# The recurrence's output turned over GpSimd's queue; gate bias and causal mask prepared by GpSimd and added by VectorE in the maximum's instruction

## The chip, the cores and the metric

The kernel runs on one core of one Trainium2 chip. The metric is the device time of one execution in microseconds (us). The engines are TensorE (PE in the rows), VectorE (DVE), ScalarE (ACT), GpSimd (POOL) and SyncE (SP), whose queue issues most DMAs.

## The reference, cut to what matters

One sequence of 256 tokens, 1024 features, float32, goes through two blocks. The second holds two token mixers side by side. The recurrence's output `o_a` is normed, multiplied with a gate and multiplied by `w_branch_a`. The other mixer is causal attention of 8 heads of width 128 with a forget gate, and the change is mostly there:

```python
c = cumsum(log_sigmoid(f_logit))            # per token and head
s = (q @ k.T) / sqrt(128) + c[query] - c[key]
s = where(key <= query, s, -inf)
p = softmax(s)                              # c[query] falls out: it is the same for a whole row
o_b = p @ v
```

So the scores of head h need one value per key, -c[key], the same for every query, and the mask.

## The kernel before, in words

Tokens lie in two tiles of 128 (`TT`); within the first tile they are in reverse order. Every weight matrix is cut into units of 128 x 2048 values, 6 slots deep. For each unit SyncE loads `raw` in two DMAs (L603), ScalarE rounds it to `high` (L1365), VectorE takes `rest` = raw - high (L1961), and TensorE does 24 products of 512 columns from them (L817 to L819 or L854 to L856), three per pair of operands. TensorE works units in a fixed order, and the other engines run programs written out by hand that name, for each unit u of the block `win2` (36 units, j = u // 2 names the product), what is done there besides. `load(u)` on SyncE first waits until unit u - 6 is used (L598); after the weights it does the small transfers listed for that unit (L604 to L608), in order, each with its wait.

A tensor is "turned" in two steps: VectorE transposes it in blocks of 32 x 32, one DMA stores it in DRAM, four DMAs read it back with the blocks exchanged (`turn`, L643).

**The attention.** At u = 7 VectorE scans the gate logits to `fcum` (40 rows; rows 0 to 7 and 32 to 39 both hold the 8 heads), clears `fbias` (L2531) and signals `fcum_ready`. At u = 8 ScalarE copies `fcum` to `fbias` in a rounded form (L1739) and VectorE puts the remainder into rows 32 to 39 (L2607). Head n is in unit u = 26 + n (`FOX_SLOT`). In `fox(n)` TensorE spreads row n and its remainder over all partitions by a product of the two-hot matrix `identr` with `fbias` (L1173, 384 columns), adds the mask by a product of the identity `identb` with `causal` (L1175, 256 columns in bf16), and adds the scores in L1178. Both are accumulated in one bank of PSUM. VectorE reduces each tile to its negated maximum (L2553, 128 and 256 columns), ScalarE exponentiates with it as bias and sums (L1811), VectorE divides at the start of the next unit (`fox_scale`, L2083 to L2089) and blocks `fpT`, which SyncE turns (L663, L667), and in `fox(n + 3)` TensorE multiplies with the values (L1186, L1187); VectorE takes the result to `fo` (L2635).

In each unit u of this stretch VectorE's order is: `fox_scale` of the head before, `rest` of unit u + 4, the maximum, the gate (L2597, odd units from 29), the second half of the output's turn (L2632, units 32 and 34), `fo`. ScalarE's is: `high` of unit u + 4, the tanh of the gate (L1770), the rounding of the turned output (L1803, units 32 and 34), the exponentials.

**The recurrence's output.** At u = 28 and 30 VectorE transposes token tile 0 and 1 from `hg` to `oa_squares` (L2640). SyncE stores each (L648) and reads it back into `hg` (L654), at `load(34)`, `load(35)` and `load(36)`, `load(37)` of the block. ScalarE makes `at_high`, VectorE `at_rest` (L2632), and TensorE waits for both tiles of `at_rest` (`oa_rest`, L1224) before the first unit of `brA`. The gate of the second branch takes the place of `oa_squares`, so VectorE waits until it is stored (L2594).

**GpSimd** issues the small loads on a queue of its own, and takes differences for the recurrence (L742 to L763), the last at some 605 us. Then it waits until the last head's product is done (L797), loads `mem` (L798) and the gains.

Of the kernel before, what the change touches and what calls it, by code (L numbers as in the profile page):

```python
# [222 lines left out]
def build(nc, dram, out_dram):  # L223
    ctx = ExitStack()
    with ctx:
# [29 lines left out]
        for name, shape, dt in (  # L255
            ("ident", [P, P], F32), ("identb", [P, P], BF16), ("causal", [P, TT, P], BF16),
# [3 lines left out]
            ("meanvar", [P, TT, 2], F32), ("identr", [P, HH], F32R), ("eps", [P, 2 + 2 * TT], F32), ("negmax", [P, HH, 2], F32),  # L260
# [3 lines left out]
        identr = small["identr"]  # L264
        partsum = small["eps"][:, 2:2 + 2 * TT].rearrange("p (a t) -> p a t", a=2)
        ident, identb, causal = small["ident"], small["identb"], small["causal"]
# [100 lines left out]
        fbias = place("fbias", [P, P + S], F32R, area + 62 * KB)  # L367
# [35 lines left out]
        mem_turn = (sem("mem_blocked"), [sem(f"mem_stored{n}") for n in range(2)], [sem(f"mem_landed{n}") for n in range(2)],  # L403
# [70 lines left out]
        eps_ready = sem("eps_ready")  # L474
        fox_blocked, fox_stored = sem("fox_blocked"), sem("fox_stored")
# [12 lines left out]
        CONSTS1, CONSTS2 = 8, 4  # L488
# [85 lines left out]
        def _(sync):  # L574
# [16 lines left out]
            def load(u):  # L591
# [16 lines left out]
                turn_probabilities(u)  # L608

# [33 lines left out]
            def turn(u, at, sems, n, home, landing=None, turns=1, ready=None, stored_at=None):  # L643
# [5 lines left out]
                if u == at + 1:  # L649
                    sync.wait_ge(stored[n], stored_at or 16 * turns)  # L650
# [23 lines left out]
            def turn_tokens(u):  # L674

                for tt in range(TT):
                    turn(u, UNIT["win2"] + 34 + 2 * tt, oa_turn, tt, oa_squares[:, tt, :], hg[:, tt, :],
                         stored_at=16 * (tt + 1))
                for tt in range(TT):
                    turn(u, UNIT["brA"] + 9, mem_turn, tt, mem_blocked[:, tt, :])  # L680
                for j in range(2):
                    turn(u, UNIT["brB"] + 7 + 2 * j, y2_turn, j, y2_blocked[j][:, :], stored_at=16 * (j + 1))
                for j in range(2):
                    turn(u, UNIT["mk"] + 7 + 2 * j, mem_turn, j, mk_blocked[:, j, :], turns=2, ready=keys_blocked(j))
# [35 lines left out]
        def _(pool):  # L720
# [15 lines left out]
            pool.dma_start(identb[:, :], dram["c_identb"]).then_inc(consts2_landed, 16)  # L736
# [68 lines left out]
        def _(pe):  # L805
# [364 lines left out]
            def fox(n):  # L1170
                if n < HH:
                    out = aux(("fs", n))
                    pe.matmul(out[:, 0:P + S], identr[:, n:n + 1].to_broadcast([P, P]), fbias[:, :], start=True, stop=False)  # L1173
                    diagonal = out[:, 0:P + S].rearrange("p (n c) -> p n c", n=3)[:, 0:3:2, :]
                    pe.matmul(diagonal, identb[:, :], causal[:, :, :], start=False, stop=False)  # L1175
                    for tt in range(TT):
                        o = out[:, 0:P] if tt == 0 else out[:, P:P + S]
                        mm = pe.matmul(o, fqT[:, n, tt * P:(tt + 1) * P], fox_tokens(fkT, n, *range(tt + 1)), start=False, stop=(tt == TT - 1))  # L1178
# [10 lines left out]
            for u in range(36):  # L1189
# [23 lines left out]
                for n in FOX_SLOT[u]:  # L1213
                    if n == 0:
# [3 lines left out]
                        pe.wait_ge(sem("fcum_rest"), 2)  # L1218
                        pe.wait_ge(consts1_landed, 16 * CONSTS1)
                        pe.wait_ge(consts2_landed, 16 * CONSTS2)  # L1220
# [122 lines left out]
        def _(act):  # L1343
# [379 lines left out]
            for u in range(36):  # L1723
# [12 lines left out]
                if u == 8:  # L1736
                    act.wait_ge(sem("fcum_ready"), 1)
                    for c0, w in ((0, P), (P, S)):
                        act.activation(fbias[0:FROWS, c0:c0 + w], fcum[:, 0:w], ACT.Copy).then_inc(sem("fcum_high"), 1)  # L1739
# [1198 lines left out]
```

## Time and profile before

| | us |
|---|---|
| median of 3 runs | 1052.24 (1051.68 to 1054.19) |
| the profiled execution | 1051.98 |
| its span, first to last instruction | 1050.2 |
| TensorE busy | 1043.2 (99%) |
| VectorE busy | 753.7 (72%) |
| ScalarE busy | 598.4 (57%) |
| GpSimd busy | 68.9 (7%) |
| mean granted TensorE clock | 0.999 of full speed |

Busy time counts an engine's instructions, not its waits. TensorE's products are pipelined: each row lasts longer than its distance to the next, and that distance is what it costs. In rows with a count (x2) the duration is that of all together. "[a <-b]" at the end of a row says that the engine stood idle a us before it, until b was done. The attention's eight heads lie between 631 and 700 us.

### The profile page before, as it was taken

What the parts mean: (1) busy time and instruction counts of PE and PEld (TensorE: products, weight loads), DVE (VectorE), ACT (ScalarE), POOL (GpSimd) and SP (SyncE); (2) the same over time, 40 slices, a digit from 0 to 9 for tenths busy, and PEclk for the clock granted to TensorE, in tenths of its full rate; (3) what the DMA queues carried; (4) which work ended last, traced back from release to release, by engine and by line L of the source; (5) the groups of instructions that cost most, each with busy time, mean ns of one, the idle gap of its engine ahead of it and who ended that gap; (6) DMA issues with size and microseconds to landing.
All of it is one profiled execution on the core that took longest, in us unless ns stands there. A gap on an engine that the chain in (4) does not pass through costs nothing.

```text
span 1050.2 us, 12947 instructions
## 1 busy us (share of the span) xinstructions
PE 1043.2 (99%) x4939; PEld 872.2 (83%) x4939; DVE 753.7 (72%) x901; ACT 598.4 (57%) x800; POOL 68.9 (7%) x59
## 2 busy tenths in 40 slices
PE   9999999999999999999999999999999999999997
PEld 7888888888888888888888888888889988888886
DVE  5768787775787675468888978868778666767642
ACT  6573776765385555448784645555366657565531
POOL 1200000000000000000434500000000000000000
PEclk9999999999999999999999999999999999999999
DMA  9934899985487777648756845979975345878741
GB/s 362 395 131 170 301 303 299 296 264 187 185 280 229 245 239 233 199 177 279 254 179 233 241 161 180 285 247 322 318 250 195 116 171 201 244 239 235 247 158 40
DMA packets 97645, 243.89 MB, mean 232 GB/s; under 512 B 15104, under 2 KB 41904, under 8 KB 97456
## 3 DMA queue, kind: packets, MB, share of 16 engines
q1 hardware_dynamic: 94016, 231.51, 67.4%
q0 software_dynamic: 3136, 11.23, 3.0%
q8 instruction: 39, 0.64, 0.2%
q10 hardware_dynamic: 432, 0.33, 0.1%
q14 instruction: 22, 0.18, 0.0%
HBM read 220.48 MB, written 22.54 MB: 231 GB/s over the span
## 4 chain that ended last, share of the span: by engine, by line
PE 98%; DVE 1%; ACT 0%; issue 0%; DVEq 0%
PE ps L817 24%; PE ps L819 24%; PE ps L818 24%; PE ps L856 5%; PE ps L854 5%; PE ps L855 5%; PE ps L951 1%; PE ps L1141 1%; PE ps L1250 1%; PE ps L1252 1%; PE ps L1251 1%; PE ps L1002 1%; PE ps L1003 1%; PE ps L913 1%; PE ps L914 1%; PE ps L912 1%
## 5 line engine op out<-in xcount | busy, mean ns | idle before, releaser
L1961 DVE TENSOR_TENSOR rest<-raw,high 128x2048 fp32r<-128x2048 f32 x129 | 296.1, 2312 | 75.8 <-ACT high L1365 75.2
L817 PE MATMUL ps<-high,xt_high 128*128 128x512 f32 x824 | 324.4, 394 | 0.2 <-DVE rest L1961 0.2
L818 PE MATMUL ps<-rest,xt_high 128*128 128x512 f32 x824 | 320.8, 389 | 0.0
L819 PE MATMUL ps<-high,xt_rest 128*128 128x512 f32 x824 | 320.8, 389 | 0.0
L1365 ACT ACTIVATE high<-raw 128x2048 fp32r<-128x2048 f32 x129 | 244.4, 1910 | 67.6 <-DMA raw<-in_units_dram 67.5
L817 PEld LDWEIGHTS ps<-high,xt_high 128*128 128x128 f32 x824 | 154.8, 188 | 32.0 <-DVE rest L1961 0.6
L819 PEld LDWEIGHTS ps<-high,xt_rest 128*128 128x128 f32 x824 | 154.7, 188 | 32.1
L818 PEld LDWEIGHTS ps<-rest,xt_high 128*128 128x128 f32 x824 | 154.8, 188 | 31.1
L1966 DVE SCALAR_TENSOR_TENSOR rest<-raw,wgain,high 128x512 fp32r<-128x512 f32 x176 | 119.1, 746 | 35.3 <-ACT high L1369 35.3
L1369 ACT ACTIVATE high<-raw,wgain 128x512 fp32r<-128x512 f32 x176 | 110.9, 716 | 9.1 <-DMA raw<-in_units_dram 9.1
L1625 ACT ACTIVATE act<-ps,recips 128x256 f32<-128x256 f32 x44 | 18.5, 471 | 85.0 <-PE ps L819 85.0
L817 PE MATMUL ps<-high,ht_high 128*128 128x512 f32 x168 | 65.4, 389 | 0.0
L818 PE MATMUL ps<-rest,ht_high 128*128 128x512 f32 x168 | 65.4, 389 | 0.0
L819 PE MATMUL ps<-high,ht_rest 128*128 128x512 f32 x168 | 65.4, 389 | 0.0
L854 PE MATMUL ps<-high,xt_high 128*128 128x512 f32 x152 | 60.5, 398 | 0.0
L856 PE MATMUL ps<-high,xt_rest 128*128 128x512 f32 x152 | 59.4, 391 | 0.0
L855 PE MATMUL ps<-rest,xt_high 128*128 128x512 f32 x152 | 59.2, 390 | 0.0
L1385 ACT ACTIVATE xt_high<-ps 128x512 fp32r<-128x512 f32 x26 | 15.2, 598 | 58.6 <-PE ps L951 53.2
L2310 DVE SCALAR_TENSOR_TENSOR hid<-ps,recips,act 128x256 f32<-128x256 f32 x44 | 19.2, 478 | 39.6 <-ACT act L1625 39.6
L817 PEld LDWEIGHTS ps<-high,ht_high 128*128 128x128 f32 x168 | 31.5, 188 | 6.6
L819 PEld LDWEIGHTS ps<-high,ht_rest 128*128 128x128 f32 x168 | 31.5, 188 | 6.5
L818 PEld LDWEIGHTS ps<-rest,ht_high 128*128 128x128 f32 x168 | 31.5, 188 | 6.5
(372 smaller groups left out, 1442.5 us busy)
## 6 DMA issues: line engine op xcount, KB each, us to landing
raw<-in_units_dram SPq DMA_DIRECT2D x350, 512.0 KB, 4.8
gv_turned<-gv_blocked SPq DMA_DIRECT2D x11, 512.0 KB, 5.2
gv_t<-gv_turned SPq DMA_DIRECT2D x44, 128.0 KB, 4.1
turned<-blocked SPq DMA_DIRECT2D x22, 256.0 KB, 5.3
hid_t<-turned SPq DMA_DIRECT2D x88, 64.0 KB, 4.1
fox_turned<-fqT SPq DMA_DIRECT2D x6, 512.0 KB, 3.9
raw<-in_units_dram SPq DMA_DIRECT2D x8, 256.0 KB, 4.8
fqT<-fox_turned SPq DMA_DIRECT2D x16, 128.0 KB, 4.1
```

The lines of the kernel that those rows point to most:

```text
L817: pe.matmul(out, sh, wh, start=first, stop=False)
L818: pe.matmul(out, sh, wr, start=False, stop=False)
L819: mm = pe.matmul(out, sr, wh, start=False, stop=last)
L854: pe.matmul(out, sh, wh, start=first, stop=False)
L855: pe.matmul(out, sh, wr, start=False, stop=False)
L856: mm = pe.matmul(out, sr, wh, start=False, stop=last)
L1365: act.activation(high[:, u % SLOTS, c], raw[:, u % SLOTS, c], ACT.Copy).then_inc(unit_high, 1)
L1369: ins = act.activation(high[:, u % SLOTS, c], raw[:, u % SLOTS, c], ACT.Copy, scale=g[:, k:k + 1])
L1625: act.activation(act_[:, j % 2, tt, :], gate_values[:, tt, :], ACT.Silu, scale=recips[:, c:c + 1])\
L1961: vec.tensor_tensor(rest[:, slot, c], raw[:, slot, c], high[:, slot, c].bitcast(F32), ALU.subtract).then_inc(unit_rest, 1)
L1966: ins = vec.scalar_tensor_tensor(rest[:, slot, c], raw[:, slot, c], g[:, q:q + 1], high[:, slot, c].bitcast(F32), ALU.mult, ALU.subtract)
L2310: ins = vec.scalar_tensor_tensor(hid[:, j % 2, :, tt, :], fold(values[:, tt, :]), recips[:, c + tt:c + tt + 1], fold(act_[:, j % 2, tt, :] ...
```

## The change

The two TensorE products per head that add bias and mask are gone. SyncE stores `fcum` in DRAM in two DMAs after `load(win2 + 13)`; ScalarE waits for them before it writes `hi`, which lies in the same place. GpSimd reads row h of it back for every head, spread over 128 partitions (192 KB in SBUF), into one of three places (`fbias`), waits for the landing, and adds the mask to the two diagonal tiles. Bias h + 2 is issued after the maximum of head h. VectorE waits for the mask of its head, and one instruction per tile then writes -(scores + bias) over the scores in PSUM and puts the minimum of it out, which is the negated maximum. The exponential takes the scores with scale -1. The clearing of `fbias`, its rounding and its remainder go, and `identr` and `identb` with their set-up.

The turn of the recurrence's output goes from SyncE's queue to GpSimd's, between the masks: tile 0 around the mask of head 4, tile 1 around that of head 6. `mem_stored` becomes one semaphore, so the first read of the turned `mem` waits for both stores.

```diff
+            def store_biases(u):
+                if u == UNIT["win2"] + 13:
+                    sync.wait_ge(sem("fcum_ready"), 1)
+                    for c0, w in ((0, P), (P, S)):
+                        sync.dma_start(fcum_dram[:, c0:c0 + w], fcum[0:HH, 0:w]).then_inc(fcum_stored, 16)
...
-                    turn(u, UNIT["win2"] + 34 + 2 * tt, oa_turn, tt, oa_squares[:, tt, :], hg[:, tt, :],
-                         stored_at=16 * (tt + 1))
-                for tt in range(TT):
-                    turn(u, UNIT["brA"] + 9, mem_turn, tt, mem_blocked[:, tt, :])
+                    turn(u, UNIT["brA"] + 9, mem_turn, tt, mem_blocked[:, tt, :], stored_at=16 * TT)
...
+            def spread_bias(h):
+                if h == 1:
+                    pool.wait_ge(aux_done, AUX["lv", 1, 128, 0][0] + 1)
+                elif h == HALF + 1:
+                    pool.wait_ge(aux_done, AUX["fs", HALF - 1][0] + 1)
+                elif h:
+                    pool.wait_ge(sem("fox_max"), TT * (h - 1))
+                pool.dma_start(bias_home(h)[:, :], fcum_dram[h].partition_broadcast(P)).then_inc(fbias_landed[h % 2], 16)
+            def mask_bias(h):
+                pool.wait_ge(fbias_landed[h % 2], 16 * (h // 2 + 1))
+                d = bias_home(h)[:, :].rearrange("p (n c) -> p n c", n=3)[:, 0:3:2, :]
+                pool.tensor_tensor(d, d, causal[:, :, :], ALU.add).then_inc(fbias_masked, 1)
+            def store_outputs(tt):
+                pool.wait_ge(oa_turn[0], tt + 1)
+                pool.dma_start(oa_turn[3][tt], oa_squares[:, tt, :]).then_inc(oa_turn[1][tt], 16)
+            def read_outputs(tt):
+                pool.wait_ge(oa_turn[1][tt], 16 * (tt + 1))
+                src = oa_turn[3][tt].rearrange("(q i) (r e) -> r i q e", q=4, r=4)
+                for r in range(4):
+                    pool.dma_start(hg[32 * r:32 * r + 32, tt, :].rearrange("p (q e) -> p q e", q=4), src[r]).then_inc(oa_turn[2][tt], 16)
...
+                    pool.wait_ge(fcum_stored, 32)
+                    pool.wait_ge(consts1_landed, 16 * CONSTS1)
+                    for h in range(2):
+                        spread_bias(h)
+                    for h in range(2):
+                        mask_bias(h)
+                    for h in range(HH - 2):
+                        spread_bias(h + 2)
+                        if h in (2, 4):
+                            store_outputs((h - 2) // 2)
+                        mask_bias(h + 2)
+                        if h in (2, 4):
+                            read_outputs((h - 2) // 2)
...
-                    pe.matmul(out[:, 0:P + S], identr[:, n:n + 1].to_broadcast([P, P]), fbias[:, :], start=True, stop=False)
-                    diagonal = out[:, 0:P + S].rearrange("p (n c) -> p n c", n=3)[:, 0:3:2, :]
-                    pe.matmul(diagonal, identb[:, :], causal[:, :, :], start=False, stop=False)
...
+                        act.wait_ge(fcum_stored, 32)
                         scaled("win2", j, hi_[:, :, c])
...
+                        vec.wait_ge(fbias_masked, n + 1)
                         for tt in range(TT):
                             c0, c1 = (0, P) if tt == 0 else (P, P + S)
-                            ins = vec.tensor_reduce(small["negmax"][:, n, tt:tt + 1], src[:, c0:c1], AX_X, ALU.max, negate=True)
-                            ins.then_inc(sem("fox_max"), 1)
+                            vec.tensor_tensor_reduce(src[:, c0:c1], src[:, c0:c1], bias_home(n)[:, c0:c1], -1.0, -3 * NEG,
+                                                     ALU.add, ALU.min, small["negmax"][:, n, tt:tt + 1])\
+                                .then_inc(sem("fox_max"), 1)
```

## Rows read from the trace of the kernel before

**Rows 1.** The page's busy us of each engine, share of the span, instructions.

```profile
PE 1043.2 (99%) x4939; PEld 872.2 (83%) x4939; DVE 753.7 (72%) x901; ACT 598.4 (57%) x800; POOL 68.9 (7%) x59
```

**Rows 2.** Who TensorE waited for: us in total, times, longest us.

```profile
PE ps L817 <- DVE rest L1961: 0.2, 1, 0.2
```

**Rows 3.** TensorE in order of time: start us, us, line, operation, [idle before].

```profile
638.23 0.34 PE L1173 MATMUL ps<-fbias,identr 128*128 128x384 f32 x1
638.41 0.28 PE L1175 MATMUL ps<-causal,identb 128*128 128x256 bf16 x1
638.53 0.82 PE L1178 MATMUL ps<-fkT,fqT 128*128 128x128 f32 x4
```

**Rows 4.** Who VectorE, then ScalarE, waited for from 636 to 691 us.

```profile
DVE expsum L2083 <- ACT fp L1811: 3.7, 3, 1.6
DVE rest L1961 <- ACT high L1365: 1.3, 3, 0.4
...
ACT gate L1770 <- DVE gate L2597: 13.7, 3, 5.3
ACT fp L1811 <- DVE negmax L2553: 12.8, 5, 4.6
```

**Rows 5.** VectorE in order of time, 635 to 691 us.

```profile
635.51 0.61 DVE L2553 TENSOR_REDUCE negmax<-ps 128x1 f32<-128x128 f32 x2
636.04 0.15 DVE L2013 RECIPROCAL recips<-roots 128x1 f32<-128x1 f32 x1
...
682.10 0.62 DVE L2553 TENSOR_REDUCE negmax<-ps 128x1 f32<-128x128 f32 x2
682.63 1.40 DVE L2597 SCALAR_TENSOR_TENSOR gate<-ps,recips,gains 128x512 f32<-128x512 f32 x2
...
687.76 2.29 DVE L1961 TENSOR_TENSOR rest<-raw,high 128x2048 fp32r<-128x2048 f32 x1 [0.44 <-ACT high L1365]
689.97 1.22 DVE L2632 TENSOR_TENSOR at_rest<-hg,at_high 128x1024 fp32r<-128x1024 f32 x1
```

**Rows 6.** ScalarE in order of time, 684 to 687 us.

```profile
684.06 1.06 ACT L1770 ACTIVATE gate<-gate 128x1024 f32<-128x1024 f32 x1 [4.21 <-DVE gate L2597]
685.03 0.35 ACT L1811 ACTIVATE fp<-ps,negmax 128x128 f32<-128x128 f32 x1
685.28 0.19 ACT L1811 ACTIVATION_READ_ACCUMULATOR fp<-ps,negmax 128x1 f32 x1
685.37 0.46 ACT L1811 ACTIVATE fp<-ps,negmax 128x256 f32<-128x256 f32 x1
...
685.82 1.91 ACT L1365 ACTIVATE high<-raw 128x2048 fp32r<-128x2048 f32 x1
```

**Rows 7.** TensorE's first brA product; its first load of mk weights.

```profile
693.22 0.47 PE L817 MATMUL ps<-high,at_high 128*128 128x512 f32 x1
...
737.44 0.19 PEld L817 LDWEIGHTS ps<-high,mt_high 128*128 128x128 f32 x1 [0.18 <-DVE mt_rest L2686]
```

**Rows 8.** GpSimd and VectorE in order of time, single rows.

```profile
463.60 0.53 POOL L800 DMA_DIRECT2D gains<-in_gain_gate_dram  x1 [0.26 <-DVE y L2026]
...
564.67 0.61 POOL L746 TENSOR_TENSOR he_cross<-hb 128x256 f32<-128x256 f32 x1
...
594.35 3.92 POOL L762 TENSOR_TENSOR he_next<-hb 128x1024 f32<-128x1024 f32 x1 [1.54 <-DVE hqk L2446]
...
596.39 4.03 DVE L1961 TENSOR_TENSOR rest<-raw,high 128x2048 fp32r<-128x2048 f32 x1
```

**Rows 9.** SyncE's queue in order of time.

```profile
665.14 0.33 SPq L648 DMA_DIRECT2D oa_turned<-oa_squares  x1
```

**Rows 10.** DMA issues: queue, count, KB each, median us to landing.

```profile
hg<-oa_turned SPq DMA_DIRECT2D x8, 128.0 KB, 5.4
...
gains<-in_gain_mem_pre_dram POOLq DMA_DIRECT2D x1, 512.0 KB, 12.3
```

**Rows 11.** ScalarE in order of time, at its first write of hi.

```profile
517.82 1.27 ACT L1670 ACTIVATE hi<-ps,recips 128x512 f32<-128x512 f32 x2 [2.35 <-PE ps L819]
```

More of the change, by code:

```diff
@@ L259, in build @@
             ("recips", [P, TT * len(NORMS)], F32), ("moments", [P, TT, 12], F32),
-            ("meanvar", [P, TT, 2], F32), ("identr", [P, HH], F32R), ("eps", [P, 2 + 2 * TT], F32), ("negmax", [P, HH, 2], F32),
+            ("meanvar", [P, TT, 2], F32), ("eps", [P, 2 + 2 * TT], F32), ("negmax", [P, HH, 2], F32),
             ("expsum", [P, HH, 2], F32), ("crossref", [P, TT * HALF], F32), ("lb", [P, 4, HH], F32), ("total", [P, TT * HALF], F32)):
@@ L263, in build @@
             at = -(-marks[name][1] // 32) * 32
-        identr = small["identr"]
         partsum = small["eps"][:, 2:2 + 2 * TT].rearrange("p (a t) -> p a t", a=2)
-        ident, identb, causal = small["ident"], small["identb"], small["causal"]
+        ident, causal = small["ident"], small["causal"]
         levelmask = small["levelmask"]
@@ L366, in build @@
         at_rest = place("at_rest", [P, KC, S], F32R, area)
-        fbias = place("fbias", [P, P + S], F32R, area + 62 * KB)
+        fbias = [place(f"fbias{n}", [P, P + S], F32, area + k * KB) for n, k in enumerate((62, 28, 54))]
         junk_m = place("junk_m", [P, TT, NB], F32, area + 8 * KB)
@@ L402, in build @@
                     nc.dram_tensor("oa_turned", (2, P, D), F32, kind="Internal").ap())
-        mem_turn = (sem("mem_blocked"), [sem(f"mem_stored{n}") for n in range(2)], [sem(f"mem_landed{n}") for n in range(2)],
+        mem_turn = (sem("mem_blocked"), 2 * [sem("mem_stored")], [sem(f"mem_landed{n}") for n in range(2)],
                      nc.dram_tensor("mem_turned", (2, P, D), F32, kind="Internal").ap())
@@ L474, in build, with bias_home @@
         eps_ready = sem("eps_ready")
+        fcum_dram = nc.dram_tensor("fcum_rows", (HH, P + S), F32, kind="Internal").ap()
+        fcum_stored, fbias_masked = sem("fcum_stored"), sem("fbias_masked")
+        fbias_landed = [sem(f"fbias_landed{n}") for n in range(2)]
+        def bias_home(h):
+            return fbias[0 if h % 2 == 0 else 1 + h // HALF]
         fox_blocked, fox_stored = sem("fox_blocked"), sem("fox_stored")
@@ L641, in turn_conv, with turn @@
                         sync.dma_start(gv_t[32 * r:32 * r + 32, j % 2, :, :], src[r]).then_inc(gv_landed[j % 2], 16)
-            def turn(u, at, sems, n, home, landing=None, turns=1, ready=None, stored_at=None):
+            def turn(u, at, sems, n, home, landing=None, ready=None, stored_at=None):
                 blocked, stored, landed, scratch = sems
@@ L683, in turn_tokens @@
                 for j in range(2):
-                    turn(u, UNIT["mk"] + 7 + 2 * j, mem_turn, j, mk_blocked[:, j, :], turns=2, ready=keys_blocked(j))
+                    turn(u, UNIT["mk"] + 7 + 2 * j, mem_turn, j, mk_blocked[:, j, :], ready=keys_blocked(j),
+                         stored_at=16 * (TT + j + 1))
             def turn_hidden(u):
@@ L1735, in _ @@
                     fox_log_sigmoids()
[L1736 to L1739, printed above, removed]
                 if u == 5:
@@ L2330, in _ @@
             ffn("upA", "downA", "ffn1_pre", "win2")
-            vec.tensor_tensor(identr[:, :], ident[:, 0:HH], ident[:, FROWS - HH:FROWS], ALU.add).then_inc(sem("identr_ready"), 1)
             vec.wait_ge(sem("wf_high"), 1)
@@ L2822, in constants @@
     tok = ORDER
-    out = {"c_ident": np.eye(P, dtype=f32), "c_identb": np.eye(P, dtype=f32).astype(np.dtype("bfloat16"))}
+    out = {"c_ident": np.eye(P, dtype=f32)}
     at = tok.reshape(TT, P)
```

22 lines of the change are left out of this document (6 added, 16 removed).

## The prediction

> **What bounds the kernel now.** I read the page's busy shares first: TensorE is busy 1043.2 of 1050.2 us [rows 1]. So an edit off TensorE is worth something only if it ends or makes a wait of TensorE. The view of who waited for whom, for TensorE, has after its first microsecond one wait of 0.2 us [rows 2]: every removed TensorE instruction is worth its own slot, as long as no other engine is then late. Third, TensorE's order of time at an attention head gives the slots: L1173 starts at 638.23, L1175 at 638.41, L1178 at 638.53 [rows 3]. Fourth, the waits of VectorE and ScalarE between 636 and 691 us, the stretch of the eight heads. They name only each other: VectorE waits for `fp` and `high` of ScalarE, ScalarE for `gate` and `negmax` of VectorE [rows 4]. Neither waits for TensorE or a DMA there, so these two run in a closed loop at their own pace. The reader should see that a loop so closed passes every added nanosecond on, and gains nothing from a faster TensorE. Last, where that loop meets TensorE again: `oa_rest`, the second L2632, starts at 689.97 and takes 1.22, so ends at 691.19 [rows 5]; the first `brA` product (L1224's wait stands before it) starts at 693.22 [rows 7]. The spare time is 2.0 us. That is the number that decides.
>
> **TensorE, removed.** Per head the bias product holds 638.41 - 638.23 = 0.18 and the mask product 638.53 - 638.41 = 0.12 [rows 3], 0.30 together; there are eight such pairs, at the same distances: -2.40 us. The load of `fqT` for L1178 can then run under the L819 in front of it, as the load for L1173 did, so I charge nothing for it. The bound below is 8 x 0.18 = 1.44 (if the load of `fqT` took the second slot), the one above 2.40. I take 2.40. TensorE would then be ready for `brA` at 693.22 - 2.40 = 690.82.
>
> **VectorE, the maximum.** Eight pairs of reductions (128 and 256 columns) become eight pairs of add-and-minimum that also read `fbias` from SBUF and write PSUM. The pair of reductions takes 0.61 [rows 5]. Per column VectorE needs (2.29 - 1.22) / 1024 = 1.04 ns, from L1961 with 2048 columns and L2632 with 1024 [rows 5], so 384 columns take 0.40 and the pair's fixed part is 0.21. The nearest two-input row with PSUM is L2597: 2 x 512 columns in 1.40, fixed part 1.40 - 1.07 = 0.33. So the least growth x of a pair is 0.12 us; below that would need a second operand from SBUF to cost nothing. How the minimum gets out is not in the trace for VectorE. On ScalarE it is an instruction of its own: L1811 at 685.03, its accumulator read at 685.28, the next L1811 at 685.37, so 0.09 each [rows 6]: x = 0.12 + 0.18 = 0.30. If it costs what VectorE's smallest operations do (L2013, 636.04, 0.15 plus a gap of 0.04 [rows 5]), x = 0.12 + 0.38 = 0.50. I take 0.22, between the first two, because nothing shows yet that VectorE needs the extra instruction; 0.12 and 0.50 are the ends.
>
> The Trainium skill, "VectorE: DVE Perf Modes", section "Two Vector instructions with no wait between them", says that an operation which also writes out its accumulator is two instructions. No row of before shows VectorE doing it. Taken at its word it makes the second rival below likelier than the forecast.
>
> All of x lies on the loop. After an odd unit it runs maximum, `gate` (L2597 at 682.63), tanh on ScalarE (684.06), exponentials (685.03), `high` (685.82), `rest` (687.76), L2632 (689.97) [rows 5, 6]; ScalarE's exponential waits for the maximum as well [rows 4]. Eight pairs stand between 635.51, the first [rows 5], and 691.19: `oa_rest` comes 8x = 1.76 us later.
>
> **GpSimd beside VectorE.** Eight masks of 128x256 are added; such an operation takes 0.61 [rows 8]. One measured collision: GpSimd's L762 starts at 594.35 and takes 3.92, and the L1961 that starts at 596.39 takes 4.03 in place of 2.29 [rows 8, 5]. VectorE lost 1.74 us, to about when GpSimd was done. A mask is at most 0.61, so the ends are 0 and 8 x 0.61 = 4.9. `rest` runs once per unit of some 6.7 us ((682.10 - 635.51) / 7 [rows 5]), and a mask must already be under way when it starts: 0.61 / 6.7 = 9% per head, average loss half a mask. Eight heads: 0.2 us. I take 0.2. Since no such row is found for most of VectorE's operations, the upper end that I keep is 1.0, five times the average; 4.9 needs every mask to hit in full.
>
> That an operation loses only when the other holds the port at its start is the Trainium skill's rule too: "SBUF — State Buffer", section "Who interferes with whom": whoever issues first gets the shared pair for the whole instruction. By it the new add-and-minimum, with one SBUF input, is never held. It also says that GpSimd's descriptor writing starves while VectorE copies in a two-port mode, which speaks against moving DMAs to GpSimd's queue. No row here shows that; it would make the last rival likelier.
>
> **SyncE's queue.** The output's store and four reads per token tile leave it, and the wait in front of the store: the store for tile 1 goes at 665.14, when VectorE's transposition is done [rows 9]. The probabilities' reads behind it go earlier. That helps no one who waits now; it keeps those reads ahead of a TensorE that comes 2.4 us sooner. New on SyncE are two small stores at unit 13: some 0.8 us by two issues (the 0.33 of [rows 9], twice, rounded up) ahead of the next weights. ScalarE's new wait for them stands before `hi`, where it now idles 2.35 us for TensorE [rows 11]; the cover holds unless the stores land over 2 us late. Price: 0.
>
> **Small removals.** ScalarE's copy of the biases, VectorE's clearing and subtraction, `identr`, one constant load: all before the heads, on engines that TensorE does not wait for: 0. The shared `mem_stored` makes the first read wait for both stores, which are issued back to back; those reads feed `mt_rest`, whose end now holds TensorE by 0.18 [rows 7], but behind VectorE's own work that starts from TensorE, so it moves along with it. Price 0, at most 0.4, one more issue.
>
> **The sum.** TensorE waits at `brA` for 691.19 + 0.15 (from a last VectorE write to a load of weights, of the size of the 0.18 in [rows 7]) + 8x + c - 690.82 = 0.52 + 1.76 + 0.20 = 2.48 us. Net: -2.40 + 2.48 = +0.1. After that wait all is timed from TensorE again. The profiled execution was 1051.98 (span 1050.2 and 1.8 around it), so 1052.1; the median shown is 1052.24, 0.26 above it, and moves likewise: **1052.3 us**. Own range: x = 0.12, c = 0 gives a wait of 1.48 and 1051.3; x = 0.50, c = 1.0 gives 5.52 and 1055.4.
>
> **Rivals.**
> *The wait does not come* (chance 0.15). If the loop has slack that I don't see, the whole 2.40 stays: 1049.8. For it: VectorE's 3.7 + 1.3 us of idle time [rows 4]. Against it: all of that is idle time inside the loop, waiting for ScalarE which waited for VectorE.
> *The minimum needs instructions of its own at 0.19* (0.13). x = 0.50: wait 0.52 + 4.0 + 0.2 = 4.72, net +2.3: 1054.6. For it: ScalarE's accumulator rows [rows 6]. Against: only that they are ScalarE's, and cheaper.
> *The bias comes late through GpSimd's queue* (0.10), the case on the other side. Bias 7 is issued behind the output's second turn: store at 665.2 at the earliest [rows 9], landing L later, four reads of 0.53 (an issue on that queue, L800 at 463.60 [rows 8]), then the bias lands another L later, then 0.61 of mask: 665.2 + 2.1 + 0.5 + 0.6 + 2L = 668.4 + 2L. It is needed at 682.10 + 7x = 683.6. With L = 5.4, as the same reads had [rows 10], it is ready at 679.2. From L = 7.6 it decides. One load on that queue took 12.3 later in the kernel [rows 10]; at L = 10, between the two rows, the bias is 4.8 late and the time 1052.3 + 4.8 = 1057.1. Against it: the load of 12.3 stood behind others of 1.5 MB together, the bias behind 0.5 MB.
>
> **Chances.** The forecast holds 0.62. Within 0.3% (3.2 us, about what this kernel's runs tell from no change) lie the forecast, the first rival and the second, 0.90 together; 0.05 of it I take off at either end. Faster, 0.05, needs more than the 2.40 there is to gain, so errors in the slots. Slower, 0.15, is the late bias and a pair still dearer than x = 0.50. The rest, 0.80, is the same. Range 1049.9 to 1055.8.
>
> **What would show it.** TensorE's heads: L1178 directly behind L819, each 0.30 shorter. A wait of TensorE at the first `brA` product for `at_rest` of VectorE, 1.5 to 5 us; if it is missing, the loop argument is wrong. VectorE's pairs per head at 0.7 to 0.9 us against 0.61, and whether an accumulator read stands behind each. VectorE idle for `fbias` of GpSimd before a pair would be the last rival. A time under 1049 would make the account of TensorE's slots wrong.

## The result, and the profile after

The changed kernel takes 1054.06 us (median of 21 runs, 1052.40 to 1058.40) against 1052.24 us (21 runs on the same chip, 1051.68 to 1057.31). The ratio is 1.0016, 95% interval [1.0008, 1.0023]: some 1.7 us slower (1.82 by the two medians), inside the 0.3% that the prediction called "same". Its runs also spread more: the middle half of them lies within 1.7 us (1053.27 to 1054.97), that of before's within 0.8 (1052.11 to 1052.93). A run over 2 us above the median of before is called long below; 10 of the changed kernel's 21 are, and 2 of before's 21. The profiled run took 1054.76 (span 1052.6), 0.7 above its median. "Read" below is the time at which a transfer's read goes out, and "landing" the time from a store's issue to it.

The page's busy time, and who TensorE waited for (us in total, times, longest), answer to [rows 1, 2]:

```profile
PE 1041.8 (99%) x4923; PEld 871.0 (83%) x4923; DVE 755.0 (72%) x913; ACT 598.2 (57%) x798; POOL 90.1 (9%) x84
```
```profile
PE ps L907 <- DVE rest L2005: 3.3, 1, 3.3
PE ps L1029 <- DVE warmth L2160: 1.1, 1, 1.1
PE ps L1236 <- DMA fpT<-fp_turned: 0.4, 1, 0.4
PE ps L870 <- DVE at_rest L2670: 0.2, 1, 0.2
```

TensorE does less, and has waits that were not there before; the large one, of 3.3 us, is at no place that the prediction looked at. (The 1.1 us for `warmth` lie in the first microsecond and were there before.) First the places that it did look at. TensorE at a head and at the first `brA` product, in order of time, against [rows 3, 7]:

```profile
637.57 0.39 PE L872 MATMUL ps<-high,xt_rest 128*128 128x512 f32 x1
637.80 0.81 PE L1228 MATMUL ps<-fkT,fqT 128*128 128x128 f32 x4
...
691.40 0.38 PE L1237 MATMUL ps<-fpT,fv 128*128 128x128 f32 x2
692.03 0.50 PE L870 MATMUL ps<-high,at_high 128*128 128x512 f32 x1 [0.25 <-DVE at_rest L2670]
```

The scores follow the weight products directly, and `brA` starts at 692.03, 1.19 us before 693.22 [rows 7]. That is 1.21 less than the 2.40 taken out. Some 0.5 of it lies at `brA`, which starts 0.63 behind L1237, where before had 0.14; most of the rest lies at the product with the probabilities of head 4 (L1236 at 678.64, 1.19 behind its scores where before had 0.65), which waits for their transfer. VectorE, at the first pair and around the last (against [rows 5]):

```profile
635.41 0.29 DVE L2596 CUSTOM_DVE_ANT_0 ps<-ps,fbias 128x128 f32<-128x128 f32 x1
635.62 0.14 DVE L2596 DVE_READ_ACCUMULATOR2_ANT negmax<- 128x1 f32 x1
635.62 0.46 DVE L2596 CUSTOM_DVE_ANT_0 ps<-ps,fbias 128x256 f32<-128x256 f32 x1
636.00 0.14 DVE L2596 DVE_READ_ACCUMULATOR2_ANT negmax<- 128x1 f32 x1
636.00 0.16 DVE L2057 RECIPROCAL recips<-roots 128x1 f32<-128x1 f32 x1
...
679.14 0.97 DVE L2131 TENSOR_SCALAR fp<-fp,expsum 128x128 f32<-128x128 f32 x2
...
686.95 0.55 DVE L2131 TENSOR_SCALAR fp<-fp,expsum 128x128 f32<-128x128 f32 x2
...
690.76 1.22 DVE L2670 TENSOR_TENSOR at_rest<-hg,at_high 128x1024 fp32r<-128x1024 f32 x1
```

A pair is followed after 636.00 - 635.41 = 0.59 us, against 636.04 - 635.51 = 0.53 in [rows 5]: 0.06 more. Each accumulator read is an instruction of its own, but starts with the instruction behind it and holds up nothing. One pair of L2131 takes 0.97 instead of 0.55, while GpSimd adds the last mask (679.27, 0.70). `at_rest` ends at 691.98, 0.79 after the 691.19 of before; counted from the first pair, 56.57 us instead of 55.68, it is 0.89. So far the change wins 1.19 us.

From there to the end it loses: the span less the start of `brA` is 1052.6 - 692.03 = 360.57 us, and was 1050.2 - 693.22 = 356.98. SyncE's queue, where memory rows, `y` and memory keys are turned (a store, and the reads of it); first before:

```profile
718.18 0.91 SPq L648 DMA_DIRECT2D mem_turned<-mem_blocked  x2
...
725.53 3.65 SPq L654 DMA_DIRECT2D mem_blocked<-mem_turned  x8
...
741.51 0.33 SPq L648 DMA_DIRECT2D y_turned<-y_blocked  x1
743.20 0.86 SPq L603 DMA_DIRECT2D raw<-in_units_dram  x2
748.42 2.26 SPq L654 DMA_DIRECT2D y_blocked<-y_turned  x4
...
759.04 1.75 SPq L654 DMA_DIRECT2D mk_blocked<-mem_turned  x4
```

and after:

```profile
716.02 1.45 SPq L656 DMA_DIRECT2D mem_turned<-mem_blocked  x2
...
726.36 3.65 SPq L662 DMA_DIRECT2D mem_blocked<-mem_turned  x8
...
742.04 0.43 SPq L656 DMA_DIRECT2D y_turned<-y_blocked  x1
742.52 2.73 SPq L610 DMA_DIRECT2D raw<-in_units_dram  x2
751.05 1.75 SPq L662 DMA_DIRECT2D y_blocked<-y_turned  x4
...
762.44 1.75 SPq L662 DMA_DIRECT2D mk_blocked<-mem_turned  x4
```

The stores go out 2.16 us earlier, their reads 0.83 later. Each store waits in this queue behind the reads of the store before, so a late read makes the next turn late. The lag is 0.53 at the `y` store (742.04), 2.63 at its read and 3.40 at 762.44: most of it is added where a store lands later than before. With SyncE late and TensorE early, weights that used to be loaded 1.7 us after the `y` store (743.20) now go right behind it (742.52), and the store lands after 9.0 instead of 6.9 us. The two are seen together; no run separates them. How it reaches TensorE: ScalarE, before,

```profile
764.66 1.15 ACT L1851 ACTIVATE mk_high<-mk_blocked 128x512 fp32r<-128x512 f32 x2 [9.65 <-DMA mk_blocked<-mem_turned]
765.72 7.32 ACT L1365 ACTIVATE high<-raw 128x2048 fp32r<-128x2048 f32 x4
```

and after:

```profile
767.08 1.15 ACT L1895 ACTIVATE mk_high<-mk_blocked 128x512 fp32r<-128x512 f32 x2 [10.48 <-DMA mk_blocked<-mem_turned]
768.14 7.31 ACT L1412 ACTIVATE high<-raw 128x2048 fp32r<-128x2048 f32 x4
```

ScalarE idles 10 us for the keys, and only behind them makes four `high` in a row with no further wait for a load. TensorE wants the first of these units' `rest` now and the keys later. VectorE's three `rest` and TensorE's first product with them, before:

```profile
767.65 6.70 DVE L1961 TENSOR_TENSOR rest<-raw,high 128x2048 fp32r<-128x2048 f32 x3 [1.04 <-ACT high L1365]
```
```profile
770.22 0.40 PE L854 MATMUL ps<-high,xt_high 128*128 128x512 f32 x1
```

The first of the three ends at 767.65 + 6.70 / 3 = 769.88, so 0.3 us were to spare (770.22 - 769.88). After, the same two start at 770.07 and 772.51:

```profile
770.07 6.70 DVE L2005 TENSOR_TENSOR rest<-raw,high 128x2048 fp32r<-128x2048 f32 x3 [1.03 <-ACT high L1412]
```
```profile
772.51 0.47 PE L907 MATMUL ps<-high,xt_high 128*128 128x512 f32 x1 [3.27 <-DVE rest L2005]
```

### The profile page after: what moved, and what is told of

Read it like the earlier page. It is cut to its first block, busy times and chain, and to the rows that moved or that the text cites. A ratio compares the mean times of both kernels' runs of the same rounds, so it can differ in the third digit from the quotient of the medians.

```text
span 1052.6 us, 12952 instructions
## 1 busy us (share of the span) xinstructions
PE 1041.8 (99%) x4923; PEld 871.0 (83%) x4923; DVE 755.0 (72%) x913; ACT 598.2 (57%) x798; POOL 90.1 (9%) x84
## 4 chain that ended last, share of the span: by engine, by line
PE 94%; DMA 2%; DVE 2%; ACT 1%; issue 1%; SPq 0%; DVEq 0%; ACTq 0%
PE ps L870 22%; PE ps L872 22%; PE ps L871 22%; PE ps L907 5%; PE ps L909 5%; PE ps L908 5%; PE ps L1004 1%; PE ps L1194 1%; DMA mem_turned<-mk_blocked 1%; PE ps L1297 1%; PE ps L1298 1%; PE ps L1299 1%; ACT high L1412 1%; DVE rest L2005 1%; DMA fpT<-fp_turned 1%
```

## The experiments

All were timed in five rounds beside the kernel before, whose median was 1051.94 in the first four, 1052.07 in the next and 1051.90 in the last. The differences below are to that median. The second figure in a row of the table is the ratio with its interval. The ratio is not worked out from the two medians, and in e3, e5 and e7 the two differ by some 0.4 us; where an interval takes in 1, no difference from before is shown. The columns behind it are of the one profiled run: start of the first head's scores ("head 0"), start of `brA`, the span less that start ("tail"), the longest wait at wout2's last block, and the landing of the probabilities' store of head 5, issued at about 674 us.

| kernel | us | ratio | head 0 | brA | tail | wait | landing |
|---|---|---|---|---|---|---|---|
| before | | | 632.09 | 693.22 | 356.98 | 0 | 3.7 |
| after | +1.82 | 1.0016 [1.0008, 1.0023] | 631.68 | 692.03 | 360.57 | 3.3 | 5.5 |
| e1_shared_sem | +1.23 | 1.0012 [1.0003, 1.0021] | 631.94 | 693.76 | 359.04 | 0.8 | 4.5 |
| e2_own_sems | +0.37 | 1.0004 [0.9995, 1.0013] | 631.37 | 691.55 | 358.15 | 0.2 | 5.5 |
| e3_no_products | -0.29 | 1.0001 [0.9993, 1.0010] | 631.17 | 691.60 | 357.40 | 0.2 | 3.8 |
| e4_filler | +1.66 | 1.0015 [1.0006, 1.0024] | 631.41 | 692.45 | 358.95 | 1.7 | 5.5 |
| e5_split_before | +0.01 | 0.9996 [0.9988, 1.0005] | 632.21 | 693.34 | 357.26 | 0 | 4.7 |
| e6_split_after | +0.13 | 1.0001 [0.9991, 1.0011] | 631.79 | 692.85 | 360.55 | 0 | 5.7 |
| e7_split_own | +0.05 | 1.0004 [0.9989, 1.0019] | 632.05 | 692.20 | 356.90 | 0 | 4.4 |
| e8_turn_sync | +3.22 | 1.0033 [1.0016, 1.0050] | 631.21 | 692.66 | 358.44 | 1.2 | 4.4 |
| e9_plain_max | +1.23 | 1.0013 [1.0001, 1.0025] | 631.66 | 695.61 | 359.09 | 1.7 | 7.2 |
| e10_no_bias_loads | +1.12 | 1.0013 [1.0004, 1.0021] | 631.54 | 691.70 | 359.20 | 1.8 | 4.2 |
| e11_split_no_products | -0.77 | 0.9994 [0.9985, 1.0002] | 631.07 | 694.31 | 356.89 | 0 | 4.3 |
| e12_bias_ahead | -0.74 | 0.9994 [0.9986, 1.0003] | 631.37 | 691.53 | 357.47 | 0 | 4.6 |

The column "head 0" is there because profiled runs differ before the attention begins. TensorE's first products stand 0.43 us apart before they stand 0.23 apart, and for a time that differs: until 6.4 us in before, while in e4 the closer spacing is reached by 5.6. So TensorE's 31st product behind its warm-up starts at 12.39 in before and at 11.72 in e4, and the difference stays until the heads:

```profile
632.09 0.82 PE L1178 MATMUL ps<-fkT,fqT 128*128 128x128 f32 x4
```
```profile
631.41 0.82 PE L1231 MATMUL ps<-fkT,fqT 128*128 128x128 f32 x4
```

Without the first head's pair of products in front (0.30), before's value would be 631.79. What a kernel wins or loses between there and `brA` is its `brA` less its head 0, not `brA` alone.

### The shared count of stores: e1 and e2

e1, on the kernel before:

```diff
-mem_turn = (sem("mem_blocked"), [sem(f"mem_stored{n}") for n in range(2)], ...
+mem_turn = (sem("mem_blocked"), 2 * [sem("mem_stored")], ...
...
-    turn(u, UNIT["brA"] + 9, mem_turn, tt, mem_blocked[:, tt, :])
+    turn(u, UNIT["brA"] + 9, mem_turn, tt, mem_blocked[:, tt, :], stored_at=16 * TT)
...
```

> The kernel before with one part of the change alone: both stores of the memory branch's turn count on one semaphore, so the first read of the turn waits for both. Theory T (the shared count puts the extra time there): the read starts 0.8 to 1.3 us later than in the kernel before, SyncE's queue carries the slip through the turns that follow, TensorE waits for a rest half at the last wout2 units, and the time is 1053.2 to 1054.7 us against 1052.2. Rival R (the stretch behind brA gives back any earlier arrival of TensorE, whatever the semaphore): the shared count alone costs nothing, 1052.0 to 1052.6 us.

e2, on the changed kernel:

```diff
-mem_turn = (sem("mem_blocked"), 2 * [sem("mem_stored")], ...
+mem_turn = (sem("mem_blocked"), [sem("mem_stored"), sem("y2_stored")], ...
...
-    ... mem_blocked[:, tt, :], stored_at=16 * TT)
+    ... mem_blocked[:, tt, :], stored_at=16)
...
```

> The changed kernel with this one part undone: the two stores of the memory branch's turn count on two semaphores (the second shares the one of the y2 turn, whose stores come later), so the first read waits for its own store only. Theory T: the saving at brA (1.2 us) stays, the 3.3 us wait at the last wout2 units goes, and the time is 1050.8 to 1051.6 us, faster than before. Rival R: as the changed kernel, 1053.5 to 1054.5 us, and the wait for the rest half is still there.

e1 is slower by 1.23 us with nothing else changed. Its read goes out at 726.82, 1.29 after 725.53, and TensorE has two waits behind `brA` that before does not have, at `mt_rest` and at wout2 (and one of 0.4 us for `fpT` ahead of it):

```profile
PE ps L817 <- DVE mt_rest L2686: 0.8, 1, 0.8
PE ps L854 <- DVE rest L1961: 0.8, 1, 0.8
```

That is the mechanism, made by that edit alone; 1053.17 is at the lower edge of theory T's range, and e1's interval, [1.0003, 1.0021], does not reach down to 1. (Its profiled run, at 1054.58, is one of its longer ones.) Taking the count out of the changed kernel brings +1.82 down to +0.37, and the wait from 3.3 to 0.2. The two agree: 1.2 and 1.45 us, though the intervals of e2 and of the changed kernel overlap. But e2 is not at the 1050.8 to 1051.6 us that theory T gave it. Its `brA` is 1.67 us earlier than before, 0.42 of which was there at the first head (631.79 less 631.37). Of the 1.25 that it wins from there to `brA`, nearly all comes back: its tail is 1.17 us longer. Rival R, wrong about the count, has a part in it.

### TensorE's slots alone: e3 and e4

e3, on the kernel before:

```diff
-    pe.matmul(out[:, 0:P + S], identr[:, n:n + 1].to_broadcast([P, P]), fbias[:, :], start=True, stop=False)
-    pe.matmul(diagonal, identb[:, :], causal[:, :, :], start=False, stop=False)
-    mm = pe.matmul(o, ..., start=False, stop=(tt == TT - 1))
+    mm = pe.matmul(o, ..., start=True, stop=True)
```

> The kernel before without the two products per head that add gate bias and causal mask (left out of the computation: gate bias and mask in the fox heads' scores), everything else as it was. It gives TensorE alone the 2.4 us. Theory T: with VectorE at its old pace the wait for at_rest at brA is 0.3 to 0.6 us, 1.8 to 2.1 us are saved there, the queue behind is as in the kernel before, and the time is 1050.2 to 1050.8 us. Rival R: the earlier arrival at brA is given back between 700 and 775 us in a wait for a transfer, and the time is 1052.0 to 1054 us.

e4, on the changed kernel:

```diff
+    filler = xt_high[:, :, :].rearrange("p k t -> p (k t)")
+    pe.matmul(out[:, 0:P + S], filler[:, 0:P], filler[:, 0:P + S], start=True, stop=True)
+    pe.matmul(out[:, 0:S], filler[:, 0:P], filler[:, 0:S], start=True, stop=True)
```

> The changed kernel with two float32r products of 384 and 256 columns put back ahead of each head's scores, on operands that are there, so TensorE again has its old length in the fox heads while every other part of the change stays. Theory T: brA starts when it did in the kernel before (about 693.2 us), the shared count still makes SyncE late, and the time is as the changed kernel's or up to 1 us above: 1053.8 to 1055.2 us. Rival R: with TensorE no earlier than before there is nothing to give back, 1052.0 to 1052.6 us.

e3, at 1051.65 us, lies between the two ranges: 0.29 us gained of 2.4 by the medians, and none by the ratio of 1.0001. In its profile `brA` starts at 691.60, 1.62 early, of which 0.62 was there at the first head. Of the 2.4 us 1.0 arrives, because TensorE now waits for the probabilities (L1183 of head 2 stands 1.97 behind the scores, not 0.65):

```profile
PE ps L1183 <- DMA fpT<-fp_turned: 1.2, 1, 1.2
```

At `brA` no wait for VectorE is seen: `at_rest` is done at 690.59, before TensorE comes. So even where VectorE has nothing new, a transfer takes a part of TensorE's saving at once. Behind `brA`, 0.4 us more go. e4 puts TensorE back: its `brA` is 0.77 early, but 0.67 of that was there at the 31st product, and the filler holds 0.29 us per head (637.54 to 637.83) where the pair held 0.30. At 1053.60 us it is nearly as slow as the changed kernel, 0.2 under theory T's range and far above R's. A TensorE made faster in the heads is thus not needed for the loss.

### The order on ScalarE and VectorE: e5, e6 and e7

The same two lines on the kernel before (e5), the changed kernel (e6) and e2 (e7):

```diff
+split_to(UNIT["wout2"] + 4)
 keys_high(0)                 # ScalarE
...
 turn_keys(1)
+split_to(UNIT["wout2"] + 4)
 keys_rest(0)                 # VectorE
```

> The kernel before with one order changed: ScalarE and VectorE make the high and rest halves of the weights of wout2's last two units ahead of the first half of the turned memory keys, not behind it. These halves stood behind a wait of ScalarE of 9.65 us for the keys' transfer, though TensorE needs them first. Theory C (the time behind 770 us is set by that transfer through ScalarE's order, with about 0.4 us to spare in the kernel before): TensorE didn't wait there in the profiled run of before, so the median stays within 0.4 us of it, 1051.5 to 1052.3 us, and fewer runs are long. Rival D (the stretch is bound by its transfers' bytes, whatever the order): 1051.9 to 1052.6 us and the same spread.

> The changed kernel with that same order changed. Theory C: the 3.3 us wait for a rest half at wout2's last block is gone although SyncE's queue is still late by the shared count (first read of the keys about 762.4), brA stays 1.2 us earlier, and the time is 1050.6 to 1051.8 us, faster than both kernels. Rival D: the late transfers stop TensorE elsewhere, and the time is 1053 to 1054.5 us.

> The changed kernel with both: the order changed, and the two stores of the memory branch on semaphores of their own. Theory C: the order alone decides, so this is as the kernel with the order alone, 1050.4 to 1051.6 us. Theory T (the shared count is the cause): 1 us or more below the kernel with the order alone.

e5 is as before, and none of its 11 runs is long (1051.40 to 1052.57). e6 takes the changed kernel from +1.82 to +0.13 (their intervals overlap, [0.9991, 1.0011] and [1.0008, 1.0023]): the late queue, with the keys' first read at 764.27, no longer costs that wait. It missed its own range by 0.4 us. Its profile is of its longest run (1055.61), so it shows what a long run has and not what the median has; the 3.3 is gone, and among others these are there:

```profile
PE ps L1236 <- DMA fpT<-fp_turned: 1.8, 1, 1.8
PE ps L1297 <- DVE xt_rest L2031: 1.5, 1, 1.5
```

e7 with both edits is no better than the order alone (+0.05 and +0.13), as theory C had it against T, though 0.5 above the range that C gave. That speaks for the shared count costing mainly through this order; the intervals of e6 and e7, 1.0 and 1.6 us to either side, are too wide to exclude the 1 us of theory T. In its profiled run (1051.32) the tail is the 356.9 us of before, with `brA` 1.02 us earlier; five of its 12 runs are at 1051.06 to 1051.33, and three are over 1054.

### The queues: e8, e10 and e12

e8, on the changed kernel:

```diff
+    for tt in range(TT):                        # SyncE
+        turn(u, UNIT["win2"] + 34 + 2 * tt, oa_turn, tt, oa_squares[:, tt, :], hg[:, tt, :], stored_at=16 * (tt + 1))
-    store_outputs((h - 2) // 2)                 # GpSimd
-    read_outputs((h - 2) // 2)
```

> The changed kernel with the recurrence output's turn (two stores, eight reads) back on SyncE's queue at its old place; gate bias and mask stay as in the change, and so does the shared count. Theory: that move has no share in the result, so this is as the changed kernel, 1053.3 to 1054.6 us. Rival: GpSimd's slower queue delays the output's reads and with them at_rest ahead of brA; then at_rest is done 0.4 us or more earlier and the time is 0.4 to 1 us less.

Wrong on both sides. With the turn back on SyncE the loss is 3.22 us, not 1.82, and 8 of 11 runs are long. So the move to GpSimd's queue does not cost anything that shows, and is rather a gain; as the two intervals overlap a little ([1.0016, 1.0050] and [1.0008, 1.0023]), that gain is likely and not shown. The profiled run, at 1053.31, is one of its shortest, so it does not say what makes the long ones. It does show a wait that the move avoids. The reads of head 2's probabilities stand on SyncE behind the reads of the output's first tile and go out at 658.14 (as they did before, at 658.11), in the changed kernel at 655.96:

```profile
655.62 2.48 SPq L662 DMA_DIRECT2D hg<-oa_turned  x4
658.14 2.10 SPq L678 DMA_DIRECT2D fpT<-fp_turned  x4
```
```profile
655.96 1.76 SPq L678 DMA_DIRECT2D fpT<-fp_turned  x4
```

TensorE, whose scores of head 5 are at 663.37 in e8 and were at 665.59 before, is there ahead of them:

```profile
665.50 0.70 PE L1235 MATMUL ps<-fpT,fv 128*128 128x256 f32 x2 [1.32 <-DMA fpT<-fp_turned]
```

In the four profiles with a wait at head 2 (e1, e3, e8, e11) the turn is on SyncE; where it is on GpSimd, the wait for `fpT`, if there is one, is at head 4 (e8 has a short one there too).

e10, on the changed kernel:

```diff
-    pool.dma_start(bias_home(h)[:, :], fcum_dram[h].partition_broadcast(P)).then_inc(fbias_landed[h % 2], 16)
+    if h in (0, 1, HALF + 1):
+        pool.memset(bias_home(h)[:, :], 0.0).then_inc(fbias_masked, 1)
-    pool.tensor_tensor(d, d, causal[:, :, :], ALU.add).then_inc(fbias_masked, 1)
```

> The changed kernel without the eight broadcast loads of the bias rows and without GpSimd's eight masks: its tiles are filled with zero once (gate bias and mask are left out of the scores), everything else stays, the shared count too. It prices the new transfers (1.6 MB between 560 and 680 us). Theory E (these loads delay the probabilities' turns at 665 to 685 us and so add to the time and its spread): no wait for fpT, landing of the probabilities' store at 674 us back from 5.4 to about 3.7 us, and 1052.2 to 1053.2 us with fewer long runs. Rival: they cost nothing, as the changed kernel, 1053.6 to 1054.6 us.

+1.12 instead of +1.82, 2 long runs of 12 instead of 10 of 21, and the landing 4.2 instead of 5.5 us. It is in theory E's range and has no wait for `fpT`, as E had it; the landing is not as forecast (3.7), and the intervals of the two kernels overlap: a price of 0.7 us for the loads and the masks is possible, not shown. The wait at wout2 is still there (1.8), as the count is.

e12, on e7, in GpSimd's queue (the lines drawn together):

```diff
     for h in range(HH - 2):
-        spread_bias(h + 2)
+        if h + 2 < HH - 1: spread_bias(h + 2)
 ...
         mask_bias(h + 2)
+        if h == 4: spread_bias(HH - 1)
         if h in (2, 4): read_outputs((h - 2) // 2)
```

> The best guess: the changed kernel with two counts for the memory branch's stores, the last wout2 halves ahead of the keys' halves, and in GpSimd's queue the last head's bias load ahead of the reads of the output's second tile, so that it doesn't run beside the probabilities' turn of head 5. Theory E: no wait for fpT at 680 us, the long runs go, 1050.8 to 1051.5 us, faster than both kernels. Rival: as without the last edit, 1051.8 to 1052.5 us.

This is the fastest complete kernel: 1051.16 us against 1051.90, no long run (1050.61 to 1053.43). Its interval [0.9986, 1.0003] takes in no change, so that it beats the kernel before is likely and not shown; against the changed kernel's [1.0008, 1.0023] it is clear. What its last edit adds to e7, 0.8 us by the medians, is within their intervals too. A wait of 0.4 us for `fpT` is still there, which theory E had denied. Of its other waits behind the first microsecond none is over 0.2 us:

```profile
PE ps L1239 <- DMA fpT<-fp_turned: 0.4, 1, 0.4
```

### The new instruction by itself, and TensorE's gain under the new order: e9 and e11

e9, on the changed kernel:

```diff
-    vec.tensor_tensor_reduce(src[:, c0:c1], src[:, c0:c1], bias_home(n)[:, c0:c1], -1.0, -3 * NEG, ALU.add, ALU.min, ...)
+    vec.tensor_reduce(..., src[:, c0:c1], AX_X, ALU.max, negate=True)
```

ScalarE's exponential loses its scale of -1 with it.

> The changed kernel with VectorE's plain maximum in place of the add-and-minimum (left out of the computation: gate bias and mask in the fox heads' scores); their rows are still loaded and masked. It prices the new instruction form by itself. From the trace after, a pair is 0.06 us longer than two reductions, 8 x 0.06 = 0.5 us. Theory (the form is cheap, the time lies in the transfers): 0.3 to 0.6 us below the changed kernel, 1053.3 to 1053.9 us. Rival (the form holds the chain at brA): 1052.0 to 1052.5 us.

e11 is e3 with the order of e5.

> The kernel before without the two products per head (gate bias and mask left out) and with the last wout2 halves made ahead of the memory keys' halves. It shows what TensorE's 2.4 us are worth when that wait can't take them back. Theory C: 1.6 to 1.8 us of them stay, 1050.1 to 1050.6 us. Rival (another wait takes them): as without the order, 1051.3 to 1052 us.

e9 comes out at 1053.13 us, just under the theory's range and over the rival's. At +1.23 us it is 0.6 below the changed kernel, near the 0.5 of eight times 0.06; the intervals overlap, so the run bounds the form's price and doesn't measure it. Its profile is of a long run (1056.48) and shows what one such run consists of. TensorE waits 3.09 us for the probabilities of head 4, whose reads went out at 671.07; in the changed kernel the same reads, from 671.36, were there at 678.64. GpSimd's reads of the output (from 670.54) and its last bias load (672.75) are under way then, and the store of head 5's probabilities takes 7.2 us in the same stretch:

```profile
671.07 1.85 SPq L678 DMA_DIRECT2D fpT<-fp_turned  x4
674.08 0.34 SPq L682 DMA_DIRECT2D fp_turned<-fpT  x1
...
681.28 1.75 SPq L678 DMA_DIRECT2D fpT<-fp_turned  x4
```
```profile
681.11 0.70 PE L1236 MATMUL ps<-fpT,fv 128*128 128x256 f32 x2 [3.09 <-DMA fpT<-fp_turned]
...
683.29 0.63 PE L871 MATMUL ps<-rest,xt_high 128*128 128x512 f32 x1
```

The wait costs more than its length. Behind it TensorE's granted clock falls: the view by stretches has 0.55 from 682 to 684 us and 0.60 from 684 to 686 (its last but two figure), and products stand 0.43 us apart instead of 0.23. From L1236 to the next one it is 7.81 us, where the changed kernel has 6.21: 1.6 us more.

```profile
682.00:684.00 2.00, 2.00 (x7) 1.59 (x6) 1.37 (x4) 0.00 (x0) 0.91 (x1) 0.55 0.46 110
```

e11, at 1051.13 us, lies between the ranges again: -0.77 us against -0.29 without the order, and its fastest runs reach 1049.85. Of 2.4 us taken from TensorE, about a third shows in the median, and its interval still takes in no change. In its profiled run (1053.04) a wait of 2.3 us for `fpT` and 1.6 us of low clock behind it took it all: the clock was 0.50 from 668 to 670 us, and from the scores of head 5 to those of head 6 it took 11.01 us (663.01 to 674.02), where 6.80 is usual.

```profile
668.00:670.00 2.00, 2.00 (x6) 1.53 (x5) 2.00 (x5) 0.13 (x1) 0.00 (x0) 0.50 0.47 131
```

## Why the prediction was right in its number and wrong in its account

**The time** was forecast as 1052.3 us, 0.1 above before; measured is 1.7 to 1.8 above. The class "same" and the range held by luck: two errors of opposite sign. Of the forecast 2.48 us of loss up to `brA` only 1.21 came, and of the 0 forecast behind it 3.59 came in the profiled run (tail 360.57 against 356.98).

**TensorE's 2.40 us.** Right: the scores start 637.80 - 637.57 = 0.23 us after the weight product in front of them, one product's spacing, and nothing stands in the freed slots. From head 0's scores to head 1's it is 6.12 us where before had 6.44.

**VectorE's maximum, 8x = 1.76 us.** This term was mis-sized. x is 0.06 us (0.5 in all), not 0.22, and under the lower end of 0.12. The bound was wrong because it compared a two-input row with a reduction and took the difference of their fixed parts for the cost of the second operand. The accumulator read, for which the second rival stood, exists and costs no time. On the Trainium skill's rule ("VectorE: DVE Perf Modes", "Two Vector instructions with no wait between them") the trace after agrees that there are two instructions, 0.46 and 0.14 us; the price of 0.19 each that the second rival put on them does not follow. That VectorE and ScalarE pass every delay on until `at_rest` fits: 8 x 0.06 plus one collision of 0.42 make 0.90, and from the first pair to the end of `at_rest` it was 0.89 longer. That they gain nothing from a faster TensorE fits too: in e3 `at_rest` ends 0.60 earlier, the 0.62 by which that run was ahead at the first head.

**GpSimd beside VectorE, 0.20.** 0.42 in one collision. That is its order of size; the place is another, L2131 and not `rest`. The pair began at 679.14 and the mask at 679.27, and the second instruction took 0.77 us (0.32 is usual), until 0.14 behind the mask's end at 679.97. Masks that began inside a `rest` were held themselves and cost VectorE nothing. The Trainium skill's rule ("SBUF — State Buffer", "Who interferes with whom"), that whoever issues first keeps the shared pair, agrees with this row.

**SyncE's queue, price 0.** The reason given beside the price was right: the move keeps the probabilities' reads ahead of an earlier TensorE. Without it TensorE waits 1.32 us for head 2's `fpT` (e8), and 1.2 in e3. With it the wait is gone at head 2 and 0.4 us long at head 4. The saving of TensorE and the move belong together; what the move is worth in the median is not shown. GpSimd's issues took 0.54 to 0.58 us each, against 0.53 [rows 8], so nothing of a starved GpSimd queue was seen in them.

**Small removals, "price 0, at most 0.4".** This is the step that failed. The first read came 0.83 us later, though its store went 2.16 us earlier, and e1 prices the count at 1.23 us (0.3 to 2.2 by its interval). The reasoning asked who waits for `mt_rest`, the next consumer, and found VectorE ahead of it. It did not ask what stands behind the read in SyncE's queue. "After that wait all is timed from TensorE again" fails with it: the turns from 716 to 765 us follow one another on SyncE, each behind the landing of the one before. Beside it the sum had no term for the transfers at all: with TensorE earlier, `fpT` is waited for, and stores land later.

**The rivals.** At `brA` the forecast had a wait of 2.48 us, and the prediction called the loop argument wrong if the wait was missing. Measured is some 0.5 (0.25 of it in the view of waits). That sign misled: the loop does pass delays on, but x was small and TensorE, held for `fpT`, came later than forecast. The first rival's account, slack in the loop, is not what happened, and its 1049.8 us did not come. The late bias did not come: the last mask ended at 679.97, VectorE wanted it at 682.83.

**What stays open.** Why stores land later when TensorE is earlier. With counts of their own the memory stores were read after 7.35 us (before), 8.8 (e2) and 8.5 (e3), so of 2.6 us that they left earlier, 1.1 to 1.4 arrived. The DMA engines were busy throughout there (mean busy share of e3 from 700 to 710 us: 1.02, of before 0.95), so crowding is a possible cause; no run separated the load in front of a store from the one behind it. Nor is it shown which part of the wider spread of the changed kernel is due to `fpT` and which to the stretch from 716 to 772 us. The clock has a part in the longest runs: the changed kernel's two over 1057 us had a mean granted clock of 0.995 and 0.997 and e8's five over 1056 us 0.996 to 0.998, where the other runs of both had 0.998 to 1.000. Whether the fall stands behind a wait for `fpT` there, as in the two profiles that show it, is not known, as those runs have no profile.

## What to carry to other kernels

A semaphore that two transfers share moves the first read to the second landing; price it not by who needs the data but by all that is queued behind that read in order. When an engine is made faster, list which transfers now arrive after it, and take the order in which a third engine serves them (halves that are wanted now behind a wait for data that is wanted later) as the place where the gain will go. Time saved in front of a chain of store, landing and reads is saved only as far as that chain moves with it. And before a shift of less than a microsecond is read from two profiled runs, compare them at a place ahead of the change: here they differed by up to 1 us there.

## What the runs showed of the hardware

- VectorE's add-and-minimum with one PSUM and one SBUF operand, which writes PSUM, took 0.29 us (128 columns) and 0.46 us (256), spaced by 0.21 and 0.38 us. Its accumulator read of 0.14 us overlaps the next instruction wholly. ScalarE's was followed after 0.09 us [rows 6].
- A mask on GpSimd of 128x256 took 0.66 to 0.70 us in three rows in which nothing held it, and 2.59 us where it began 0.2 us into a `rest` of VectorE (646.37, 2.25). Either can be held. GpSimd's row of the held one:

```profile
646.57 2.59 POOL L809 TENSOR_TENSOR fbias<-fbias,causal 128x256 f32<-128x256 f32 x1 [3.85 <-DMA fbias<-fcum_rows]
```

- A store of the same 192 KB at the same place was read 3.7 us after its issue in the kernel before and 7.2 us in a long run of e9.
- TensorE's granted clock fell to its lower level (0.50 to 0.60 of full speed over 2 us) behind idle stretches of 2.35 us (e11, products 0.43 us apart from 667.45 on) and 3.09 us (e9, from 682.43 on), after a microsecond of products at full pace. It cost 1.6 us in both. Behind the 3.27 us of the changed kernel's wait at wout2 it stayed at 1.00, so the length of the wait alone does not decide it.
